# Adding up the squares of three state-space groups on VectorE before the product with ones

## The reference, cut to what matters

```python
    y = y.reshape(b, s, D_INNER) * jax.nn.silu(z.astype(jnp.float32))
    y = y.reshape(b, s, SSD_GROUPS, D_INNER // SSD_GROUPS)
    y = y * lax.rsqrt(jnp.mean(y * y, axis=-1, keepdims=True) + RMS_EPS)
```

## Time and profile before

| what | value |
|---|---|
| median of the 3 timed runs | 1438.11 us (1435.24 to 1438.3) |
| the profiled execution's own time | 1437.31 us |
| its span in the trace | 1435.5 us |
| mean granted TensorE clock | 0.966 of full |
| TensorE busy | 1333.7 us, 93% |
| VectorE busy | 1029.6 us, 72% |
| ScalarE busy | 869.9 us, 61% |

### The profile page before, as it was taken

One profiled execution on the slowest core, in us unless ns is written; L12 is line 12 of the kernel. 1 busy time (PEld: TensorE's weight loads), 2 busy tenths in 40 slices (PEclk: granted clock), 3 DMA queues, 4 the chain that ended last, 5 costly groups with the idle time before them and its releaser, 6 DMA issues.

```text
span 1435.5 us, 23771 instructions
## 1 busy us (share of the span) xinstructions
PE 1333.7 (93%) x9400; PEld 1224.9 (85%) x9400; DVE 1029.6 (72%) x1552; ACT 869.9 (61%) x1275; POOL 69.0 (5%) x64
## 2 busy tenths in 40 slices
PE   6989999997999998999999699899997999999993
PEld 5978999996999997999999688899995777777772
DVE  6666555566555557798977787576558999999994
ACT  4554544454444444676555566465447899999993
POOL 0000100000100000000001000010000111111113
PEclk9989999999999999999999799999998999999997
DMA  7542556552555552655444523545363899999973
GB/s 253 182 157 98 157 181 195 180 178 87 161 192 175 182 163 75 190 160 164 146 123 116 197 89 118 176 147 164 131 242 127 329 370 359 354 361 370 352 269 111
DMA packets 149164, 279.26 MB, mean 195 GB/s; under 512 B 13417, under 2 KB 121806, under 8 KB 135630
## 3 DMA queue, kind: packets, MB, share of 16 engines
q1 hardware_dynamic: 142158, 271.13, 55.0%
q0 software_dynamic: 6912, 6.84, 1.7%
HBM read 274.26 MB, written 21.50 MB: 206 GB/s over the span
## 4 chain that ended last, share of the span: by engine, by line
PE 71%; DVE 18%; ACT 6%; issue 3%; DMA 1%; ACTq 0%; DVEq 0%; POOLq 0%; POOL 0%; SPq 0%
PE psum L851 18%; PE psum L852 17%; PE psum L853 17%; DVE weights_parts L2580 4%; DVE weights_parts L2007 3%; PE psum L1389 2%; PE psum L1388 2%; PE psum L1387 2%; ACT weights_parts L1871 2%; PE psum L1412 2%; DVE arena L2381 2%; PE psum L1414 1%; PE psum L1413 1%; ACT squares L1937 1%; ACT xnorm_parts L1913 1%
## 5 line engine op out<-in xcount | busy, mean ns | idle before, releaser
L2007 DVE TENSOR_TENSOR weights_parts<-ring,weights_parts 128x1024 fp32r<-128x1024 f32 (+3 forms) x312 | 359.0, 1169 | 202.9 <-ACT weights_parts L1450 202.3
L851 PE MATMUL psum<-xnorm_parts,weights_parts 128*128 128x256 f32 x1508 | 435.6, 289 | 24.6 <-DVE xnorm_parts L2023 16.2
L1450 ACT ACTIVATE weights_parts<-ring 128x1024 fp32r<-128x1024 f32 (+3 forms) x312 | 309.6, 1010 | 203.2 <-PE psum L853 203.0
L852 PE MATMUL psum<-xnorm_parts,weights_parts 128*128 128x256 f32 x1508 | 428.3, 284 | 0.0
L853 PE MATMUL psum<-xnorm_parts,weights_parts 128*128 128x256 f32 x1508 | 427.8, 284 | 0.0
L851 PEld LDWEIGHTS psum<-xnorm_parts,weights_parts 128*128 128x128 f32 x1508 | 287.6, 191 | 33.3 <-issue 26.0
L852 PEld LDWEIGHTS psum<-xnorm_parts,weights_parts 128*128 128x128 f32 x1508 | 287.7, 191 | 1.2 <-issue 1.0
L853 PEld LDWEIGHTS psum<-xnorm_parts,weights_parts 128*128 128x128 f32 x1508 | 288.0, 191 | 0.3
L851 PE MATMUL psum<-hidden_parts,weights_parts 128*128 128x256 f32 x640 | 182.3, 285 | 0.0
L852 PE MATMUL psum<-hidden_parts,weights_parts 128*128 128x256 f32 x640 | 180.6, 282 | 0.0
L853 PE MATMUL psum<-hidden_parts,weights_parts 128*128 128x256 f32 x640 | 180.6, 282 | 0.0
(11 more groups left out here) (399 smaller groups left out, 2325.0 us busy)
## 6 DMA issues: line engine op xcount, KB each, us to landing
expert_raw<-in_w_exp_down SPq DMA_DIRECT2D x35, 1024.0 KB, 7.5
ring<-in_mlp_w_up SPq DMA_DIRECT2D x32, 1024.0 KB, 5.5
ring<-in_mlp_w_down SPq DMA_DIRECT2D x32, 1024.0 KB, 4.9
ring<-in_w_in SPq DMA_DIRECT2D x30, 1024.0 KB, 5.4
ring<-in_w_exp_gate SPq DMA_DIRECT2D x23, 1024.0 KB, 5.3
ring<-in_w_exp_up SPq DMA_DIRECT2D x23, 1024.0 KB, 7.4
ring<-in_attn_w_qkv SPq DMA_DIRECT2D x12, 1024.0 KB, 5.4
expert_raw<-in_w_exp_gate SPq DMA_DIRECT2D x12, 1024.0 KB, 5.2
```

The source lines that it names most:

```text
L851: pe.matmul(out, lh, rh, start=start, stop=False, **more)
L852: pe.matmul(out, lh, rl, start=False, stop=False, **more)
L1450: ins = act.activation(high, src, ACT.Copy)
L2007: ins = dve.tensor_tensor(low, src, high.bitcast(F32), ALU.subtract)
```

## The change

In groups g of 1, 2 and 3, VectorE adds the four tiles of squares in place, in two instructions: tiles 2 and 3 onto 0 and 1 (128x512), then tile 1 onto tile 0 (128x256). It does so after `z_silu(2g+1)`, ahead of feed B. A new semaphore `gated_folded` counts both. TensorE makes one product of ones with tile 0 where it made four, at the same place. The sum of the last gated group, `norm_sum(13)`, stays as it was.

```diff
@@ tensor engine, groups 1 to 3
                     gate_chunk(2 * g)
-                    norm_sum(9 + g)
+                    b = open_bank("norm", 9 + g)
+                    pe.wait_ge(s["gated_folded"], 2 * g)
+                    pe.matmul(bank(b)[:, 0:TOK], ones, sq[:, 0, :], start=True, stop=True).then_inc(full[b], 1)
                 gate_chunk(2 * g + 1)
@@ vector engine
                 dve.tensor_tensor(eac, eac, cg, ALU.mult).then_inc(s["cs_ready"], 1)
                 z_silu(2 * g + 1)
+                if g:
+                    dve.wait_ge(s["sq_ready"], SQ_NO[9 + g] + 2)
+                    dve.tensor_tensor(sq[:, 0:2, :], sq[:, 0:2, :], sq[:, 2:4, :], ALU.add).then_inc(s["gated_folded"], 1)
+                    dve.wait_ge(s["gated_folded"], 2 * g - 1)
+                    dve.tensor_tensor(sq[:, 0, :], sq[:, 0, :], sq[:, 1, :], ALU.add).then_inc(s["gated_folded"], 1)
                 feed(2)
```

More of the change, by code:

```diff
@@ L501, in build_two_blocks @@
             "final_ready", "before_ready", "nat_copied",
-            "sq_ready", "xn_ready", "dve_step", "att_max", "exp_done", "p_ready", "rope_done", "hid_ready",
+            "sq_ready", "xn_ready", "dve_step", "att_max", "exp_done", "p_ready", "rope_done", "gated_folded", "hid_ready",
             "gate_silu", "z_high", "z_low", "srec_ready", "p_second", "dt_ready", "conv_done", "xw_ready", "cs_ready", "ea_ready", "dec_ready",
```

## The result

The changed kernel took 1427.78 us in the median of 7 runs (1425.74 to 1431.69), the kernel before 1435.94 us (1435.24 to 1438.3) beside it: a ratio of 0.9941, 95% interval 0.9928 to 0.9955. The changed kernel measured once more, in another set, gave 0.9945 (0.9933 to 0.9958). The 1438.11 us that I forecast from was the median of three runs; the seven here have 1435.94 us, so 2.2 us of the distance between 1434.2 us and the result lie in the kernel before.

A forecast was written before the change was run, and what follows sets the result against it. The prediction took TensorE, never idle from 692.5 to 775.5 us, to bound the groups. From 1438.11 us, -3.9 on TensorE and 0 on VectorE gave 1434.2 us, range 1431.2 to 1438.0 us.

The forecast's parts named there:

- The removed products: In groups 1 to 3, three of four ones products go from TensorE: 1.30 us a group, 3.9 us off in all.
- The additions: Two on VectorE in each of groups 1 to 3, about 1.15 us a group, 3.4 us in all, costing nothing.
- the waits that I named: VectorE's waits at feeds B, C, D and the latents, 0.26 to 4.38 us each, were to hide its added work.
- VectorE's lead into group 2: Its decays at the start of group 2 lose 0.8 of 1.7 us slack before TensorE's broadcasts; it holds.
- The stage behind moves as a whole: After 775.57 us, ScalarE then VectorE work to 804.09 us starts when TensorE finishes the groups, so restart near 800.2 us.
- The rival of a lost part: A later stage (expert-stage DMA, or the 788 to 804 us wait) keeps half the gain: 1436.1 us, chance 0.2.
- the clock rival: Behind the groups, each further low-clock stretch after idle time takes back 2.7 us; one or two: chance 0.06, three: 0.03.
- the sum 3.9 + 0: Over the whole kernel: -3.9 us on TensorE, 0 on VectorE; the full gain had chance 0.63.

The follow-up runs named there:

- one_product_no_adds: The kernel before with one ones product, of the first tile of squares alone, in groups 1 to 3 and no additions on VectorE: 1427.98 us, ratio 0.9929.

## Why the prediction was wrong

*The removed products*: 6 records of 0.216 us in three groups, 3.9 us. Measured 3.8 us on the chain (4.0 at 800.09 us less the 0.2 from before the groups). Right.

*The additions*: hidden, by the waits that I named. Right in place and in size, shown by the chain without them, equal to 0.01 us, and by the kernel that has them and four products (0.9998). VectorE's lead into group 2 and the decays there did not make TensorE wait: it is busy for all of the 79.20 us of the groups.

*The stage behind moves as a whole*: right until 800.09 us.

*The rival of a lost part*: it did not come; DMA at 0.92 in that stretch gave nothing back.

*The step that failed* is in the clock rival: "the idle times stay as long as before, so I expect the same stretches." The idle times did stay (4.45, 3.49, 4.32, 6.34 us), the stretches didn't: 42 us at the low clock became 24. I had priced a stretch rightly, 2.7 us, and let it move the time only upwards and with 0.09 in all. It moved it down, by 4.3 us in the medians and 6.3 in the profiled execution, and the sum 3.9 + 0 had no term for it. I took the kernel's low clock for a property of the length of its idle times, when executions with the same idle times had 42, 35 or 24 us of it. The size of the removal was right, so that the direction came true is no luck; the 4.3 us on top I had not foreseen at all. The Trainium skill (TensorE: Matmul & The Clock Gate, on the HAM clock gate) says that its timing does not start with the kernel; I read that as noise with no mean. Single executions agree with the page: two of the changed kernel restarted at 800.09 and 800.38 us and had 24 and 35 us of low clock, and its runs spread from 1425.74 to 1431.69 us. But the medians did not stay at the shift: at 3.9 us they lie beyond it in all four measurements, 0.9929 to 0.9945, where 0.9973 would be the shift alone.

What stays open: why each stretch comes out short or long, and why the kernels gain more at a shift of 3.9 us than at 3.0. In the first profile stretches shortened when TensorE restarted at 800.09 instead of 804.09 us, but one_product_no_adds restarted at the same 800.09 us and kept the long ones. Two things are shown: the part beyond 3.9 us is not the edit's, since the same time taken off elsewhere brings it too, and in the traces it goes with the clock in the stretches behind. That the time of the restart decides is not shown.

## What to carry to other kernels

Where TensorE restarts after idle times of some microseconds, a change of a few microseconds ahead of them is measured as that change plus what the clock then does, which may be larger than the change itself: here 3.9 us taken off gained 8.2, and 0.87 us put back lost 4.6. Before crediting an edit, compare the granted clock of the stretches behind it, and take the same time off at another place: if that gains as much, the rest isn't the edit's. Moving a sum from the busy engine to one that waits is worth what the chain shows, here 1.3 us a group.

## What the runs showed that I had not expected

The lead grew at each restart, 4.0, 5.3, 6.3, 7.7, 10.0 us, without any of the waits getting shorter by more than 0.4 us. And products of zeros in idle times were worth 6.3 us to the kernel before but only 0.7 us to the changed one, though they took 18 us of low clock out of it as well. How much low clock there is says little without where it falls.
